# A recurrence whose small products run in 64x64 tiles of the array, with its states kept plain

## What is computed

```python
def wkv_scan(r, decay, k, v, a_vec, b_vec, s0, reverse):
    def step(s, inp):
        r_t, w_t, k_t, v_t, a_t, b_t = inp
        sa = jnp.einsum('bhvk,bhk->bhv', s, a_t)
        s = s * w_t[:, :, None, :] + sa[..., None] * b_t[:, :, None, :] + v_t[..., None] * k_t[:, :, None, :]
        return s, jnp.einsum('bhvk,bhk->bhv', s, r_t)
...
# 16 heads of size 64; 2 directions; first over 256 context rows (only the final state counts), then over 256 rows of x
wlog = (w0[d] + jnp.tanh(xw @ w1[d]) @ w2[d])      # decay logits
decay = jnp.exp(-jnp.exp(-jax.nn.softplus(-wlog) - 0.5))
a = jax.nn.sigmoid(a0[d] + (xa @ a1[d]) @ a2[d])
```

## Time and profile before

| | us |
|---|---|
| median of three runs | 2922.94 |
| lowest and highest | 2915.03, 2923.7 |
| span of the profiled execution, first to last instruction | 2917.6 |
| of it, the recurrence's inputs end and its first products run | 2016 to 2044 |
| of it, the rounds of the recurrence | 2044 to 2411 |
| of it, output and second experts | 2411 to the end |

### The profile page before, as it was taken

The page is one execution under the profiler, slowest core; times in us unless marked ns, Lnnn a source line. Parts: engine busy times, 40 slices in busy tenths (PEclk is TensorE's granted clock), DMA queues, the critical chain, the costliest instruction groups (busy, mean ns, idle before and its releaser), DMA issues.

```text
span 2917.6 us, 56415 instructions
## 1 busy us (share of the span) xinstructions
PE 2663.8 (91%) x24182; PEld 1779.7 (61%) x24182; DVE 1366.9 (47%) x1878; ACT 983.7 (34%) x1705; POOL 189.3 (6%) x195
## 2 busy tenths in 40 slices
PE   8999999999999999999999998899999989766666
PEld 6877877878878878875433333344778865332222
DVE  5776566877866567643100001423777773000001
ACT  4435655444446555531200100202555542000000
POOL 0102000000002000000000000002333310000000
PEclk9999999999999999999999999999999999987787
DMA  8764335776763347642899999822100017999997
GB/s 304 274 258 161 127 131 210 302 267 244 297 236 135 125 166 286 229 176 107 346 421 421 421 421 421 328 81 101 42 11 17 11 47 282 421 421 421 421 419 323
DMA packets 103997, 716.99 MB, mean 246 GB/s; under 512 B 11949, under 2 KB 14381, under 8 KB 19801
## 3 DMA queue, kind: packets, MB, share of 16 engines
q1 hardware_dynamic: 93016, 663.75, 57.8%
q10 hardware_dynamic: 10752, 49.81, 4.5%
HBM read 711.65 MB, written 1.86 MB: 245 GB/s over the span
## 4 chain that ended last, share of the span: by engine, by line
PE 61%; DMA 20%; DVE 10%; ACT 6%; issue 2%; SPq 0%; ACTq 0%; DVEq 0%
DMA weight_ring<-in_stream 20%; PE banks L2130 9%; PE banks L667 7%; PE banks L669 6%; PE banks L668 6%; PE banks L1960 3%; PE banks L2495 3%; PE banks L1103 3%; PE banks L1105 2%; PE banks L1104 2%; PE banks L2539 2%; ACT front L1371 2%; PE banks L1263 1%; PE banks L2935 1%; PE banks L2021 1%
## 5 line engine op out<-in xcount | busy, mean ns | idle before, releaser
L2130 PE MATMUL banks<-weight_ring,scratch 128*32 128x256 f32 (+1 forms) x4256 | 560.3, 507 | 148.6 <-DMA weight_ring<-in_stream 147.0
L2130 PEld LDWEIGHTS banks<-weight_ring,scratch 128*32 128x32 f32 (+1 forms) x4256 | 183.1, 129 | 505.9 <-DMA weight_ring<-in_stream 258.7
L664 DVE TENSOR_TENSOR split_high<-weight_ring,split_high 128x1024 fp32r<-128x1024 f32 x198 | 242.5, 1238 | 124.0 <-ACT split_high L659 121.8
L659 ACT CAST split_high<-weight_ring 128x1024 fp32r<-128x1024 f32 x198 | 206.8, 1052 | 272.8 <-PE banks L669 199.3
L2281 DVE TENSOR_TENSOR scratch<-scratch,banks 128x512 f32<-128x512 f32 (+1 forms) x32 | 17.8, 555 | 561.5 <-PE banks L2130 561.5
L1463 DVE TENSOR_TENSOR split_high<-weight_ring,split_high 128x1024 fp32r<-128x1024 f32 x128 | 160.2, 1262 | 160.9 <-ACT split_high L1356 160.8
L667 PE MATMUL banks<-split_high,features_low 128*128 128x512 f32 x480 | 189.9, 396 | 0.2 <-DVE resid L700 0.2
L669 PE MATMUL banks<-split_high,features_high 128*128 128x512 f32 x480 | 187.1, 390 | 0.0
L668 PE MATMUL banks<-split_high,features_high 128*128 128x512 f32 x480 | 186.8, 389 | 0.0
L1356 ACT CAST split_high<-weight_ring 128x1024 fp32r<-128x1024 f32 x128 | 133.0, 1049 | 150.1 <-PE banks L1105 144.2
L2190 ACT ACTIVATE scratch<-banks 128x512 f32<-128x512 f32 (+1 forms) x32 | 15.7, 491 | 477.7 <-PE banks L2130 477.7
(11 more groups left out here) (448 smaller groups left out, 4870.2 us busy)
## 6 DMA issues: line engine op xcount, KB each, us to landing
weight_ring<-in_stream SPq DMA_DIRECT2D x628, 1024.0 KB, 9.8
scratch<-in_kept ACTq DMA_DIRECT2D x24, 1024.0 KB, 7.6
scratch<-in_pair_rows ACTq DMA_DIRECT2D x8, 448.0 KB, 3.7
scratch<-in_kept ACTq DMA_DIRECT2D x6, 512.0 KB, 5.5
scratch<-in_lora ACTq DMA_DIRECT2D x2, 1536.0 KB, 9.3
front<-in_gain_rows ACTq DMA_DIRECT2D x5, 512.0 KB, 3.7
bias<-bias_rows SPq DMA_DIRECT2D x1, 2304.0 KB
scratch<-in_routing ACTq DMA_DIRECT2D x1, 1040.5 KB, 4.9
```

Source lines behind the costliest of these rows:

```text
L659: act.copy(split[i % 4][0], source(i)).then_inc(*self.rounded.up())
L664: dve.tensor_tensor(lo, source(i), hi.bitcast(F32), ALU.subtract).then_inc(*self.rest.up())
L2130: last = pe.matmul(self.psum[q * M:(q + 1) * M, (GATE, UP, DOWN)[part], 0:W], left, w[j][:, q * W:(q + 1) * W], start=(k == 0), stop=(k == ...
```

## The change

Five edits, all in `rwkv_scan`.

- **States.** `Sbd` is gone, with its clearing by GpSimd and the wait for it. `S` holds seven plain states of 128 partitions by 64 columns; ScalarE writes each by one instruction. `step` reads all its states from `S`.
- **y_state** is two products of 64x64, one for each head (`h`), where it was one of 128x64. Head 1 waits on a new semaphore, `y_begun`, that head 0's product has ended. In the order the two are kept apart by other work: the one of head 1 stands behind the next group.
- **Logits.** Each product with 128 weight columns is two with 64.
- **Running sums** (L2853): one 128x128 product with 512 moving columns is two, on the diagonal quarters.
- **Chunk sums** (L2856): four 128x128 products with 2 moving columns are sixteen 64x64 with 1 moving column, written to two banks; ScalarE's exponential of them reads two banks, and the order of `PC` follows.

```diff
-        S = tiles(take(3 * HD), 3)
+        take(3 * HD)
...
-        Sbd = tiles(take(4 * P), 4)
+        S = tiles(take(7 * HD), 7)
+        take(HD)
...
                 for t in range(4):
-                    for n, hid in enumerate((self.whid, self.ahid)):
-                        rows = half(d ^ n)
-                        last = pe.matmul(self.psum[:, F[n], cols(t)], hid[rows, cols(t)], self.lora2[rows, n, cols(i)],
-                                         start=True, stop=True)
-                        if t == 3:
-                            last.then_inc(*(w_logits, a_logits)[n].up())
+                    for c in range(2):
+                        for n, hid in enumerate((self.whid, self.ahid)):
+                            rows = half(d ^ n)
+                            last = pe.matmul(self.psum[half(c), F[n], cols(t)], hid[rows, blk(2 * t + c)], self.lora2[rows, n, cols(i)],
+                                             start=True, stop=True)
+                            if t == 3 and c == 1:
+                                last.then_inc(*(w_logits, a_logits)[n].up())
...
-                pe.matmul(self.psum[:, F[2], :], incl_sum[d], th_w, start=True, stop=True).then_inc(*sums_incl.up())
+                for c in range(2):
+                    last = pe.matmul(self.psum[half(c), F[2], :], incl_sum[d][half(c), half(c)], th_w[half(c), :], start=True, stop=True)
+                last.then_inc(*sums_incl.up())
                 pe.wait_ge(a_added.sem, u + 1)
                 for t in range(4):
-                    last = pe.matmul(self.psum[:, F[1], 2 * t:2 * t + 2], th_w[:, cols(t)], self.halves, start=True, stop=True)
+                    for h, c in quads:
+                        last = pe.matmul(self.psum[half(h), F[c], t:t + 1], th_w[half(c), blk(2 * t + h)], self.halves[half(c), c:c + 1],
+                                         start=True, stop=True)
                 last.then_inc(*sums_all.up())
...
-            def y_state(u, s):
+            def y_state(u, s, h):
                 t, c = order[u % 2][s]
-                pe.wait_ge(state_ready.sem, 7 * u + s)
-                ins = pe.matmul(self.psum[half(c), Y, cols(t)], HT[:, (2 * t + c) * HD:(2 * t + c + 1) * HD], Sbd[:, s - 4, :],
-                                start=False, stop=False, skip_group_check=True)
-                if s == 7:
+                if h == 0:
+                    pe.wait_ge(state_ready.sem, 7 * u + s)
+                else:
+                    pe.wait_ge(y_begun.sem, 4 * u + s - 3)
+                ins = pe.matmul(self.psum[half(c), Y, t * P + h * HD:t * P + (h + 1) * HD], HT[half(h), blk(2 * t + c)],
+                                S[half(h), s - 1, :], start=False, stop=False, skip_group_check=True)
+                if h == 0:
+                    ins.then_inc(*y_begun.up())
+                elif s == 7:
                     ins.then_inc(*y_ready.up())
...
-                if s == 3:
-                    act.wait_ge(sbd_cleared.sem, 1)
-                    if u:
-                        act.wait_ge(y_ready.sem, u)
-                if s < 3:
-                    last = act.activation(S[:, s, :], self.psum[:, BB + c, blk(t)], ACT.Copy,
-                                          scale=PC[:, u % 4, 2 * t + c:2 * t + c + 1])
-                else:
-                    for h in range(2):
-                        last = act.activation(Sbd[half(h), s - 3, half(h)], self.psum[half(h), BB + c, blk(t)], ACT.Copy,
-                                              scale=PC[half(h), u % 4, 2 * t + c:2 * t + c + 1])
-                last.then_inc(*state_ready.up())
+                if s == 3 and u:
+                    act.wait_ge(y_ready.sem, u)
+                at_ = 4 * c + t
+                act.activation(S[:, s, :], self.psum[:, BB + c, blk(t)], ACT.Copy, scale=PC[:, u % 4, at_:at_ + 1])\
+                    .then_inc(*state_ready.up())
...
-                if s == 2:
-                    pool.wait_ge(scored_kr.sem, 1)
-                    pool.memset(Sbd, 0.0).then_inc(*sbd_cleared.up())
```

More of the change, by code:

```diff
@@ L2798, in rwkv_scan @@
              "lakv_saved z_saved gw_saved mt_saved").split())
-        (ka_halved, t1_ready, nk_begun, nk_ready, rkr_ready, kk_added, bon_ready, eye_placed, sbd_cleared) = map(sem, (
-             "ka_halved t1_ready nk_begun nk_ready rkr_ready kk_added bon_ready eye_placed sbd_cleared").split())
+        (ka_halved, t1_ready, nk_begun, nk_ready, rkr_ready, kk_added, bon_ready, eye_placed, y_begun) = map(sem, (
+             "ka_halved t1_ready nk_begun nk_ready rkr_ready kk_added bon_ready eye_placed y_begun").split())
         rows_loaded = sem("even_rows_loaded"), sem("odd_rows_loaded")
@@ L3005, in step @@
                 for h in range(2):
-                    before_it = S[half(h), s - 1, :] if s < 4 else Sbd[half(h), s - 4, half(h)]
-                    last = pe.matmul(self.psum[half(h), BB + c, blk(t)], MT[half(h), c, t, :], before_it, start=False, stop=False, skip_group_check=True)
+                    last = pe.matmul(self.psum[half(h), BB + c, blk(t)], MT[half(h), c, t, :], S[half(h), s - 1, :],
+                                     start=False, stop=False, skip_group_check=True)
                 last.then_inc(*stepped.up())
-            def y_state(u, s):
+            def y_state(u, s, h):
                 t, c = order[u % 2][s]
-                pe.wait_ge(state_ready.sem, 7 * u + s)
-                ins = pe.matmul(self.psum[half(c), Y, cols(t)], HT[:, (2 * t + c) * HD:(2 * t + c + 1) * HD], Sbd[:, s - 4, :],
-                                start=False, stop=False, skip_group_check=True)
-                if s == 7:
+                if h == 0:
[7 more added lines that the diff above has]
+                elif s == 7:
                     ins.then_inc(*y_ready.up())
@@ L3047, in _ @@
                 if e is not None:
-                    y_state(e, 6)
+                    y_state(e, 5, 1)
+                    y_state(e, 6, 0)
                 if b is not None:
@@ L3053, in _ @@
                     lak_values(l)
+                if e is not None:
+                    y_state(e, 6, 1)
+                if l is not None:
                     z(l, 2)
+                if e is not None:
+                    y_state(e, 7, 0)
                 if b is not None:
@@ L3057, in _ @@
                 if e is not None:
-                    y_state(e, 7)
+                    y_state(e, 7, 1)
                 if l is not None:
@@ L3095, in _ @@
                     step(b, 4)
-                    y_state(b, 4)
+                    y_state(b, 4, 0)
                 if f is not None:
                     scores_ab(f)
+                if b is not None:
+                    y_state(b, 4, 1)
                 if l is not None:
@@ L3102, in _ @@
                     step(b, 5)
-                    y_state(b, 5)
+                    y_state(b, 5, 0)
                 if f is not None:
@@ L3346, in decays @@
                 act.wait_ge(sums_all.sem, u + 1)
-                act.activation(PC[:, u % 4, :], self.psum[:, F[1], 0:8], ACT.Exp, bias=self.decay_bias[:, 6:7], scale=0.5 * CS)\
+                act.activation(PC[:, u % 4, :].rearrange("p (c t) -> p c t", c=2), self.psum[:, F[0]:F[1] + 1, 0:4], ACT.Exp,
+                               bias=self.decay_bias[:, 6:7], scale=0.5 * CS)\
                     .then_inc(*pc_ready.up())
```

## The result

The change makes the kernel slower by 7.0 us, **2929.96 us** median of 7 runs (2926.25 to 2934.7) against 2922.94 (2915.03 to 2925.97), a ratio of 1.0029 with a 95% interval of 1.0016 to 1.0041. The profiled execution took 2926.25 us.

What follows compares the result with a forecast made beforehand. Fetching TensorE's instruction blocks was taken to bound the full rounds. 2917.6 + 9.8 - 1.5 - 0.5 + 0.7 - 1.0 = 2925.1 us, +7.5, or 2930.4 on the median of the runs; range 2905 to 2943.

Steps and rivals of the forecast that it cites:

- The bound: Full rounds: TensorE waits for its program, fetched in blocks of 256 instructions; a round takes 22.65 us.
- rival A: Full rounds: fetching is no limit, so the saved array work shows and the time is 2899 us; chance 0.14.
- The turn-around, 3.775 us: TensorE's program: time from one instruction block to the next when fetching limits, taken from six blocks of the kernel before.
- rival B: TensorE's program: a fetch can keep up 3.52 us a block, a round takes 21.1, the time is 2912 us; chance 0.10.
- The twelve rounds, +9.8 us: Full rounds: 6.0 blocks at 3.775 us make 22.65 us a round, 0.82 more than before.
- The array's work, 1.8 us less a round: TensorE's array in a full round: y_state saves 1.08 us, logits 0.24, sums 0.50.
- From there to the transposes: Ahead of the rounds, logits and sums of two units among long products: 0.74 us saved for each, -1.5 us.
- The round and a half up to the full rounds: First two rounds, half empty, where TensorE waits for VectorE and ScalarE: -0.5 us, between 0 and -1.5.
- The last rounds up to the end of the output gates: Last rounds: only the y_states add records, some 24, a fifth of a block: +0.7 us.
- C: Rounds: longer stops make the granted clock fall, 16 us more, time 2946 us; chance 0.08.
- The end, from the last round's products to the next stage: Last unit's steps: four states shorter, -1.2 us, against +0.2 for head 1's waits; -1.0 us in all.
- D: Smaller products don't run side by side: up to 0.9 us a round more in the logits, no change in time unless fetching is no limit.

Runs made afterwards that it cites:

- the padded kernel before: 24 products a unit (48 records, 1 moving column) that nobody reads, added to the kernel before the change; ratio to before 1.0102.
- the two with waits: The changed kernel with 96 or 48 already satisfied wait instructions a unit added between the two kinds of sums; ratios to before 1.0591 and 1.0281.
- the narrow pad: The changed kernel with 12 products a unit (24 records of 64x64, 1 moving column) that nobody reads, added ahead of the chunk sums; ratio to before 1.0068.

## Why the prediction was right, and where only by luck

**The bound.** "Nearly every block would be ended by the fetch": right. The stops stand on the grid of 127, there is one packet for a block, every stop over 0.35 us ends 1.2 to 1.6 us after a packet has landed, and 256 columns instead of 1 in 24 records made 0.14 us of a round of 23.4. The Trainium skill ("Runtime: NRT & Kernel Launch", Instruction fetch mechanics) calls the crossing mostly hidden, which was rival A; here it is open at five blocks of six, by 0.7 to 1.5 us in the timeline above. In the kernel before it was rarer and shorter than the prediction says: its "0.6 to 1.1 us" are 0.19 to 0.85 in the rows that it cites, and only 11 of some 67 block ends of the rounds have a stop over 0.35 us.

**The turn-around, 3.775 us.** Measured 3.757 in the changed kernel. Six blocks of the trace of before had given it, and it was a lucky pick: the eight blocks between them, from 2205.87 to 2237.75, took 31.88 us, 3.985 each. The value holds all the same, for it is the median of all packets of before, 3.76. Single distances go down to 3.30, and so below rival B's 3.52, but they are not kept up.

**The records.** 762 predicted, 9156/12 = 763 found. 6.0 x 3.757 = 22.54, and the rounds took 22.55.

**The twelve rounds, +9.8 us.** Measured +8.6; the 0.018 us by which a turn-around is shorter make the difference over 72 blocks.

**The array's work, 1.8 us less a round.** About 1.7. The logits go from 2163.46 to 2164.36, 0.90 for the estimated 0.94. The sums go from 2167.72 to 2169.16, 1.44 for the 1.4 forecast; L2861's 26 records from 2168.63 to 2169.10 stand 0.018 us apart. (The Trainium skill's "TensorEngine Tiling (Array Packing)", Instruction Overhead, has 60 cycles for each, an estimated 0.025; the trace is below it.) A y_state takes 0.12 (2162.88 to 2163.00) where I had 0.10. In the full rounds none of it reaches the time.

**Outside the full rounds** the single terms were off, and they made up for each other.

- Ahead of the recurrence I had nothing, rightly, for no line there was changed. Yet at the first product that the change touches the changed kernel is already 1.54 us early, which is scatter of the 2000 us before it:

```profile
2008.36 1.16 PE L2843 MATMUL banks<-scratch 64*128 64x128 f32 x16
```

```profile
2006.82 1.10 PE L2845 MATMUL banks<-scratch 64*64 64x128 f32 x32
```

- From there to the transposes, with the logits and sums of two units between long products, I had -1.5, and it is 26.20 - 26.59 = **-0.4** (before, then changed):

```profile
2008.36:2034.95 26.59, 26.59 (x101) 13.58 (x101) 8.94 (x13) 9.45 (x15) 12.53 (x11) 1.00 0.09 24
```

```profile
2006.82:2033.02 26.20, 26.20 (x186) 12.34 (x186) 8.94 (x13) 9.55 (x15) 12.52 (x11) 1.00 0.09 25
```

- The round and a half up to the full rounds: -0.5 predicted, 43.90 - 42.84 = **+1.1** measured. The whole stretch shown above holds 120 records more (1188 for 1068), and the clock was lower, 0.89 for 0.92. So the start of the recurrence, -2.0 in the forecast, was +0.7.
- The last rounds up to the end of the output gates: +0.7 predicted, 64.38 - 60.04 = **+4.3** measured. This term was mis-sized twice. I had counted 24 more records, of the y_states alone, and 65 were there (1748 for 1683), since the stretch opens with the last unit's sums: half a block, 1.9 us. And the clock stood at half for 13.7 us of it instead of 3.4, by the granted clock of the two stretches, 0.89 and 0.97. So C's fall of the clock did come, in a place where I had not looked for it; what it cost there no run shows by itself.
- The end, from the last round's products to the next stage: -1.0 predicted, 12.06 - 13.16 = -1.1. Here ScalarE's single instruction for a state is on the path (L3385, 84 of them in the twelve rounds, mean 319 ns), but the clock, 0.72 for 0.68, has a part that I could not take apart.
- What follows the recurrence I had at nothing. It took 2924.5 - 2423.97 = 500.5 us against 2917.6 - 2412.96 = 504.6, **-4.1**. No line of it was changed. In the eleven kernels of the experiments, which touch nothing there either, it took between 499.1 and 503.1, so the profiled execution of before was simply at the long end.

The sum of the parts is -1.5 + 0.7 + 8.6 + 4.3 - 1.1 - 4.1 = +6.9, and the forecast was +7.5. The term that carries it was right in mechanism and nearly in size. That the total agrees so closely is luck. In this pair of executions the recurrence itself, from its first logits to the next stage, takes 417.2 us against 404.6, **+12.6**, where I had forecast +7.5, and stretches that the change doesn't touch give 5.7 back by scatter. The runs, 7.0 us in the median with an interval from 4.7 to 12.0, say that 12.6 is too much: the one profiled execution of before seems to have a recurrence some us shorter than most. Against it the recurrence of each of the eleven other kernels, too, is longer than the ratio of their runs gives, by 0.4 to 9 us. How much of the start and the tail is the change's own is thus open.

**The rivals.** A falls with the first timeline. B falls with the distances: 3.52 is not kept up. C didn't come in the full rounds of the change (clock 1.00), but came in those of seven other kernels, the padded kernel before and the two with waits above all, and in the change's own last rounds. D: the small products do run side by side, as the spacing of L2845 and L2861 shows.

**What stays open.** Why the clock falls where it does. The padded kernel before was busy for 272.14 of 284.43 us and had 0.96; the change was busy for 219.64 of 270.61 and had 1.00. No run here separates the shapes from the places of the stops. The same holds for the long distances: the change took away wide products and also brought the round to six whole blocks, and the nearest to only one of the two are the padded kernel before (six blocks with the old products, 28 long distances) and the narrow pad (the new products with 6.19 blocks, 18 long ones, a mean of 3.772). Nor is it settled whether the change with the old logits is better than the change. No version beat the kernel before, except by leaving work out. A version with fewer passes for each product was not tried.

## What to carry to other kernels

Where an engine stops in the midst of its own work with "issue" as the only reason, count the instructions between two stops and look for the queue of instruction packets: if both give the same block, the engine's program is being fetched too slowly, and its time is at least the number of blocks by the turn-around. Under that bound, by the pads here, an edit is priced by instructions added, not by columns saved: merging products should pay where the block has time to spare, and splitting them only where a block's own work is longer than a fetch, though no kernel here has won by either. And before a part is taken back because it "costs records", ask how long the block will be that it comes to stand in.

## What the hardware showed that I had not expected

- 24 records with 256 columns and with 1 column cost the same 0.8 to 0.9 us a round, while TensorE's busy time differed by 10.4 us in twelve rounds.
- A wait that is satisfied already costs TensorE's program 0.098 us an instruction when 96 stand in a row (0.089 with 48), six to seven times the 0.0145 us between two narrow matmuls. I had it at nothing.
- The next packet of instructions starts only some 1.2 us after TensorE has gone on with the block before, and it is 2.5 us from a packet's start to the end of the stop (medians of 60 stops). The two make the 3.76 us.
- The clock fell for 3.4 us in seven of twelve rounds of a kernel in which TensorE was busy for 96% of the time, and never in the rounds of one that was busy for 81%.
